# Three helpers of a float32 decoder block: five matmuls whose completion TensorE no longer waits for

## The reference

```python
hs = concatenate([meta, x])                                   # 272 x 2048
hs = hs + 0.5 * swiglu(rmsnorm(hs, ffn1_norm), w_gate1, w_up1, w_down1)     # width 5632
h  = rmsnorm(hs, mix_norm)
u  = h @ w_in + b_in                                          # 2048 -> 5 x 1024: b, c, v, a, g
y_sc = b * causal_dwconv(c * v, conv_sc_w)                    # 3 taps
z    = causal_dwconv(a * sigmoid(g), conv_cf_w) + conv_cf_b   # 31 taps
y_cf = silu(layernorm(z, ln_cf_g, ln_cf_b))                   # over 1024 channels
hs = hs + concatenate([y_sc, y_cf]) @ w_out
hs = hs + 0.5 * swiglu(rmsnorm(hs, ffn2_norm), w_gate2, w_up2, w_down2)
out = rmsnorm(hs, final_norm)[16:]

def rmsnorm(x, g):      return x * rsqrt(mean(x * x) + 1e-6) * g
def layernorm(x, g, b): return (x - mean(x)) * rsqrt(var(x) + 1e-6) * g + b
def swiglu(h, wg, wu, wd): return (silu(h @ wg) * (h @ wu)) @ wd
```

## Time and profile before

| | |
|---|---|
| median of 3 runs | 1862.93 us (1862.60 to 1865.21) |
| the profiled execution's own time | 1862.93 us |
| its span, first to last instruction | 1861.1 us |
| TensorE (PE) busy | 1848.4 us, 99% |
| VectorE (DVE) busy | 1087.9 us, 58% |
| ScalarE (ACT) busy | 902.9 us, 49% |
| mean granted TensorE clock | 0.999 |

### The profile page before, as it was taken

The page is one execution under the profiler, slowest core; times in us unless marked ns, Lnnn a source line. Parts: engine busy times, 40 slices in busy tenths (PEclk is TensorE's granted clock), DMA queues, the critical chain, the costliest instruction groups (busy, mean ns, idle before and its releaser), DMA issues.

```text
span 1861.1 us, 34888 instructions
## 1 busy us (share of the span) xinstructions
PE 1848.4 (99%) x14425; PEld 1803.5 (97%) x14425; DVE 1087.9 (58%) x1218; ACT 902.9 (49%) x1151; POOL 5.9 (0%) x17
## 2 busy tenths in 40 slices
PE   9999999999999999999999999999999999999998
PEld 8999999999999999999999999999999999988886
DVE  7545445555554454468899987555555555544454
ACT  6443434343433443359988765444444444444443
POOL 1000000000000000000000000000000000000000
PEclk9999999999999999999999999999999999999999
DMA  6655555555555565555656566666666666666664
GB/s 222 193 172 177 173 176 174 175 174 176 175 175 176 175 179 173 180 164 178 182 186 177 182 196 194 199 192 192 192 192 194 194 193 195 214 189 189 194 189 135
DMA packets 283359, 342.29 MB, mean 184 GB/s; under 512 B 10639, under 2 KB 223985, under 8 KB 283152
## 3 DMA queue, kind: packets, MB, share of 16 engines
q1 hardware_dynamic: 282672, 340.44, 59.6%
q10 hardware_dynamic: 320, 0.53, 0.1%
q0 software_dynamic: 288, 0.19, 0.0%
HBM read 339.02 MB, written 2.10 MB: 183 GB/s over the span
## 4 chain that ended last, share of the span: by engine, by line
PE 98%; DVE 1%; DMA 0%; ACT 0%; SPq 0%; issue 0%; DVEq 0%
PE ps L463 28%; PE ps L464 28%; PE ps L465 28%; PE ps L558 4%; PE ps L557 4%; PE ps L556 4%; DMA x_tok<-in_x 0%; DVE w_lo L866 0%; PE ps L425 0%; PE ps L574 0%; DVE zc L1067 0%; PE ps L580 0%; DVE ln_mu L892 0%; SPq L320 0%; PE ps L479 0%; ACT o_tok L852 0%
## 5 line engine op out<-in xcount | busy, mean ns | idle before, releaser
L866 DVE TENSOR_TENSOR w_lo<-raw,w_hi 128x1024 fp32r<-128x1024 f32 x639 | 781.5, 1224 | 711.3 <-ACT w_hi L641 709.3
L641 ACT ACTIVATE w_hi<-raw 128x1024 fp32r<-128x1024 f32 x639 | 677.0, 1061 | 915.5 <-PE ps L465 764.4
L463 PE MATMUL ps<-x_hi,w_hi 128*128 128x272 f32 (+2 forms) x3456 | 976.6, 283 | 1.4 <-DVE x_lo L875 1.2
L464 PE MATMUL ps<-x_lo,w_hi 128*128 128x272 f32 (+2 forms) x3456 | 975.9, 282 | 0.0
L465 PE MATMUL ps<-x_hi,w_lo 128*128 128x272 f32 (+2 forms) x3456 | 972.0, 281 | 0.0
L463 PEld LDWEIGHTS ps<-x_hi,w_hi 128*128 128x128 f32 x3456 | 648.9, 188 | 2.8 <-PE ps L479 1.4
L464 PEld LDWEIGHTS ps<-x_lo,w_hi 128*128 128x128 f32 x3456 | 650.7, 188 | 0.0
L465 PEld LDWEIGHTS ps<-x_hi,w_lo 128*128 128x128 f32 x3456 | 649.7, 188 | 0.0
L464 PE MATMUL ps<-a_lo,w_hi 128*128 128x272 f32 x704 | 202.4, 287 | 0.0
L465 PE MATMUL ps<-a_hi,w_lo 128*128 128x272 f32 x704 | 202.2, 287 | 0.0
L463 PE MATMUL ps<-a_hi,w_hi 128*128 128x272 f32 x704 | 201.9, 287 | 0.0
(11 more groups left out here) (139 smaller groups left out, 828.3 us busy)
## 6 DMA issues: line engine op xcount, KB each, us to landing
raw<-in_ffn_w_up SPq DMA_DIRECT2D x176, 512.0 KB, 4.4
raw<-in_ffn_w_down SPq DMA_DIRECT2D x176, 512.0 KB, 4.8
raw<-in_ffn_w_gate SPq DMA_DIRECT2D x175, 512.0 KB, 4.4
raw<-in_w_in SPq DMA_DIRECT2D x80, 512.0 KB, 3.5
raw<-in_w_out SPq DMA_DIRECT2D x32, 512.0 KB, 4.7
x_tok<-in_x SPq DMA_DIRECT2D x4, 512.0 KB, 7.9
gain_tok<-in_final_norm SPq DMA_DIRECT2D x1, 1024.0 KB, 5.1
out_y<-o_tok SPq DMA_DIRECT2D x2, 512.0 KB, 2.9
```

What stands on the lines that cost most here:

```text
L463: pe.matmul(dst, w_high, act_high, start=first, stop=False)
L464: pe.matmul(dst, w_high, act_low, start=False, stop=False)
L641: act.activation(w_hi[s][:, :], raw[s][:, :], ACT.Copy).then_inc(hi_ready, 1)
L866: dve.tensor_tensor(w_lo[s][:, :], raw[s][:, :], w_hi[s][:, :].bitcast(F32), ALU.subtract).then_inc(lo_ready, 1)
```

## The change

Three lines are taken out, one in `square_sums` and two in `layernorm_sums`. Since `square_sums` is called three times, five waits go. The matmuls, their order and the semaphores that they raise stay, and so do the waits of VectorE on them and TensorE's later waits on what VectorE has read.

```diff
             def square_sums(norm, phase):
                 pe.wait_ge(sum_ready[norm], 5 if norm == "start" else KD)
                 pe.matmul(ps[:, 7, 0:width[phase]], ones[:, :], sq_sum[:, tokens(phase)],
                           start=True, stop=True).then_inc(stats_done[norm], 1)
-                pe.wait_ge(stats_done[norm], 1)
...
                     pe.matmul(ps[:, 0, SEQ:2 * SEQ], ones[:, :], ln_sum[:, :],
                               start=True, stop=True).then_inc(ln_mean_done, 1)
-                    pe.wait_ge(ln_mean_done, 1)
                 if b == 10:
                     pe.wait_ge(ln_var_sum, 1)
                     pe.wait_ge(emptied, banks_before("out_sc", 2))
                     pe.matmul(ps[:, SET, SEQ:2 * SEQ], ones[:, :], ln_sum[:, :],
                               start=True, stop=True).then_inc(ln_var_done, 1)
-                    pe.wait_ge(ln_var_done, 1)
```

## The result

The changed kernel is slower: 1880.01 us (1879.94 to 1882.21, 4 runs) against 1864.07 us, a ratio of 1.0088 with a 95% interval of 1.0073 to 1.0104. The 1864.07 is the middle of four runs that lie in two pairs, 1862.60 and 1862.93, 1865.21 and 1865.26; in the later experiments the kernel before took 1862.6 to 1862.7. The forecast was 1861.6 us, in a range of 1860.5 to 1863.8. The five stalls are gone, and each of the five places is shorter by about what was forecast. But behind the sum matmul of gu2, TensorE went through the rest of the stage at a slower pace, and that cost 18 us.

What follows compares the result with a forecast made beforehand. TensorE, busy 1848.4 of 1861.1 us, was taken as the bound. Gains of 0.97 us (gu1, ag, gu2) plus 0.325 (out_sc) made 1.30 off 1862.93, so 1861.6 us, range 1860.5 to 1863.8.

Steps and rivals of the forecast that it cites:

- The working of one site: At each of the five sum matmuls, the stretch from first pass to L464 shortens by 0.325 us, 1.63 in all.
- The three points that could have taken something away: At each site: met wait costs nothing, float32 to fp32r no price, load may not pass ahead; bounds 0 and 0.49 us.
- Rival A: At the five sites the gap stays, since load or matmul can't start before the second pass ends: 1862.7 us, chance 0.10.
- after it TensorE has no wait until the end: Behind gu2's sum matmul TensorE waits for nothing, so that site's 0.325 us reaches the end.
- a loss below zero has no mechanism here: no instruction is added or moved: At one site, the gain was taken as at least 0 and at most 0.49 us.
- the 0.325 that L603 should have come earlier: In out_sc, L603 comes 0.325 us earlier, so VectorE's L1060 starts near 1070.83; of two sites, one counts.
- the waits for `w_lo`, forecast to grow from 0.82 to 1.15 us: At the end of out_sc, the gain behind L603 ends in TensorE's longer wait for VectorE's two `w_lo` blocks.
- The start at 1083.26: TensorE's start after the `w_lo` waits in out_sc, set by VectorE; it moves by what L1060 moves, 0.325 us.
- rival B: In out_sc VectorE swallows more: only gu2 counts, 1862.6 us, or three sites count, 1862.0; chance 0.13 together.
- The prediction's own sign of rival B, a move of less than 0.8: The forecast is wrong by B if TensorE's start near 1083 moves by less than 0.8.
- C: Rival: the granted clock falls to half after out_sc's longer `w_lo` wait; 6 us at that level gives 1867.6; chance 0.02.
- the chance of 0.03 for slower: For the whole kernel, slower by more than 0.2% got 0.03, faster by more 0.03, within 0.94.

Runs made afterwards that it cites:

- experiment 1: The changed kernel with the wait behind the sum matmul of gu2 put back, the other four still away: 1861.95 us, ratio 0.9978.
- experiment 12: The kernel before with only the waits in gu1 and ag taken out: 1861.76 us, ratio 0.9995.
- experiment 6: The kernel before with gu2's wait moved one block later, where it is already met: 1880.98 us, ratio 1.0098.
- experiment 2: The kernel before with only the wait behind the sum matmul of gu2 taken out: 1880.58 us, ratio 1.0098.
- experiment 3: The changed kernel plus one stall on TensorE's own matmul after block 5 of gu2's first group: 1862.16 us in one run, 1880.06 to 1882.43 in four.
- experiment 8: The changed kernel plus stalls behind blocks 4 to 7 of gu2's first group: five runs 1863.45 to 1863.75 us, five 1881.21 to 1881.72.
- experiment 9: The kernel before plus one plain float32 matmul of 128 columns after block 5 of gu2's first group, nobody waiting: 1862.82 us, ratio 0.9995.
- experiment 4: The kernel before plus one plain float32 matmul of 256 columns after block 5 of gu2's first group, nobody waiting: 1881.21 us, ratio 1.0100.
- experiment 10: The kernel before plus two plain float32 matmuls of 256 columns after block 5 of gu2's first group, nobody waiting: 1863.42 us, ratio 1.0004.
- experiment 16: The changed kernel with gu2's sum matmul issued twice in a row, nobody waiting: 1862.09 us, ratio 0.9995 against the kernel before.
- experiment 13: The kernel before with gu2 reading its moving operand from tiles with rows of 272, as stage b does: 1876.69 us, ratio 1.0073.
- experiment 14: The changed kernel with gu2's moving operand 192 bytes lower: 1889.93 us, ratio 1.0143.
- experiment 15: The kernel before, all waits kept, with gu2's moving operand 192 bytes lower: 1891.85 us, ratio 1.0154.

## Why the prediction was wrong

**The working of one site was right.** Forecast 0.325 us for each; the stretch went from 0.91 to 0.58 and from 0.87 to 0.54, so 0.33. The three points that could have taken something away (a met wait, the passage from float32 to fp32r, the load ahead of the pass) took nothing from the site itself. Rival A, and with it the rule of the Trainium skill ("TensorE: Matmul & The Clock Gate", "Part 3: Packing small matmuls — row/col tiling") that a load overlaps matmuls in flight only where row groups differ, is refuted a second time: the load at 1139.75 starts inside a pass that lasts until 1140.13, both over all 128 rows.

**The failing step is the next one**, "after it TensorE has no wait until the end", and with it "a loss below zero has no mechanism here: no instruction is added or moved". The sum carried gu2 as 0.325 us won and the 4128 matmuls behind the site at nothing; measured, they took 18.3 us more. I took the distance of 0.113 us as a property of a 256-column matmul. The profile before held two rows that speak against that, and I did not ask about them. Stage b has 256 columns as well and ran slower. TensorE's stretches of stage b and of the start of out_sc, before:

```profile
1018.00:1038.00 20.00, 20.00 (x172) 1.00 0.60 184
1042.00:1054.00 12.00, 12.00 (x108) 1.00 0.37 113
```

20 us with 172 matmuls and 12 us with 108, less two or three for the edges: 118 and 114 ns: same engine, same clock, same columns, two paces. A kernel that is bound by TensorE to 98% has its time in the product of pace and count, and a change near the stream should be asked first whether it can touch the pace. 4.5 ns is 4% of a pace, and the stage has 4128 matmuls behind the site.

**out_sc.** There too the wait's absence led into the slow pace. In the changed kernel the distances between the mean's matmul and the variance's are at 118 ns (1068.49 to 1069.20 are six in 0.71 us):

```profile
1068.49 0.28 PE L463 MATMUL ps<-y_both,w_hi 128*128 128x256 f32 x1
...
1069.20 0.28 PE L463 MATMUL ps<-y_both,w_hi 128*128 128x256 f32 x1
...
1069.55 0.59 PE L601 MATMUL ps<-ln_sum,ones 128*128 128x256 f32 x2
...
1070.18 0.42 DVE L1057 TENSOR_SCALAR step<-ps 128x256 f32<-128x256 f32 x1 [0.46 <-PE ps L601]
```

So the 0.325 that L603 should have come earlier were eaten on the way: 96 matmuls x 4.5 ns = 0.43. VectorE's wait for it did not shrink (0.35 before, 0.46 after). Behind L603 the stream stayed at 118 ns, which took up what that site gave, until TensorE waited for `w_lo`; behind those waits it was fast again. The count of matmuls from 1072 to 1079 us and from 1084 to 1100 us was 65 and 143 before; after:

```profile
1072.00:1079.00 7.00, 6.93 (x59) 1.00 0.56 193
1084.00:1100.00 16.00, 16.00 (x144) 1.00 0.77 250
```

So the waits for `w_lo`, forecast to grow from 0.82 to 1.15 us, did not grow:

```profile
1078.69 0.19 PEld L463 LDWEIGHTS ps<-y_both,w_hi 128*128 128x128 f32 x1 [0.27 <-DVE w_lo L863]
1082.29 0.19 PEld L463 LDWEIGHTS ps<-y_both,w_hi 128*128 128x128 f32 x1 [0.77 <-DVE w_lo L863]
```

By the weight loads' records they are 1.0 us in all before and 0.27 + 0.77 = 1.04 after. (The 0.82 of the prediction adds a load's idle time, 0.24, to a matmul's, 0.58.) What these two waits did, and the prediction did not foresee, was to end the slow pace in out_sc after seven blocks; gu2 has no such wait.

The start at 1083.26 moved to 1082.29, 0.97 us, which looks like the forecast of 0.975 to the digit, and is not. The changed kernel's profiled run was 0.41 ahead already at the first sum matmul (34.73 against 35.14), before any edit takes effect, because the first load of `x` landed sooner (4.84 us instead of 5.24). Net of that, 0.56 were won until there: the two sites in gu1 and ag (0.65), less 0.1 from out_sc (0.325 - 0.43). The prediction's own sign of rival B, a move of less than 0.8, is passed by the 0.97 and not by the 0.56. Experiments 1 and 12 agree: with gu1 and ag alone 0.9 was won, with both waits of out_sc gone as well 0.7. Two starts in two runs are compared only after what separates the runs before the first edit is taken off.

**Between 1083 and gu2** nothing was won or lost: gu2's sum matmul starts at 1139.54 instead of 1140.50, 0.96 earlier. From there the 18.3 us are lost.

**The same in all traces.** out_sc is a second place to look at, and eighteen traces show it. Its block 6, ahead of the first sum matmul there, starts in all of them with a first distance 0.03 to 0.06 us longer than usual (1055.62 to 1055.77 in experiment 6, 1056.11 to 1056.26 before), and in six of them (2, 3, 6, 8, 9, 12) the rest of the block is at 118 ns, in the twelve others it is at 113 or back there within a few matmuls. No edit stands ahead of this place in experiments 2, 6 and 9. Behind a sum matmul of out_sc with its wait the pace was fast in 23 of 24 cases, and four of the five streams that came to it slow left it fast (2, 9, 12 and, at the variance's, 6); behind one without it the pace was slow in 10 of 12 cases. The one slow case with a wait is experiment 6, behind the mean's matmul; before and there:

```profile
1061.00:1070.00 9.00, 9.00 (x82) 1.00 0.59 199
```

```profile
1060.00:1069.00 9.00, 9.00 (x78) 1.00 0.65 208
```

So the wait makes the fast pace likely and not certain, and a break of 0.04 us is enough to change it.

**The rivals.** B (VectorE swallows more) describes out_sc rightly in its result, three sites instead of four, but for another reason. C, the only slower case, was a fall of the granted clock; it is 1.00 in every stretch of gu2 and 0.999 over the span. "A loss below zero has no mechanism" was a statement about the instruction list, and the chance of 0.03 for slower rested on it.

**What is shown and what is open.** Shown: two steady paces at this operand position (experiments 2, 4 and 6, and 8 within one run); that one removed wait carries the whole loss (1, 2); that a stall, not the waiting instruction, separates the two (6); that a break in the rhythm of another shape gives the other pace (9, 10, 16), and a stall can go both ways (3, 8); that the pace depends on where the moving operand lies (13 to 15), though not on that alone (13). Open: what inside the chip makes a pace of 118 hold for 470 us; and why the stall behind the sum matmul of gu2 led to the fast pace in 79 of 82 runs of the kernel before, to judge by their times, while stalls behind a block did so in 6 of 15 (experiments 3 and 8). The two are not alike: the weight load stood idle for 0.46 to 0.49 us in the first and for 0.25 or 0.26 in four of the five that were traced of the second, and the stream reached the first at the fast pace and the second at either. The three runs in 82 of the kernel before at 1883 us fit the slow pace in size, but no trace of one was taken, so that is argued and not shown.

## What to carry to other kernels

Where TensorE bounds a kernel, compute the distance between matmul starts for each stage and compare stages of the same width: unequal distances with no wait and a full clock are a gain or a loss that no list of waits shows. A wait that looks superfluous may be what starts a long steady stream in its better pace, as gu2's did here, so a change next to such a stream has to be measured over the stream, not over the wait. And a kernel whose runs fall into two groups should be profiled in both before single microseconds are counted.

## What the runs showed of the hardware that was not expected

- A stream of weight load and 256-column fp32r matmul has steady distances of 113, 117, 118 or 120 ns at the same granted clock, by the position of the moving operand and by how the stream was last interrupted; 113 and 118 occur at one and the same position (gu2's tiles, and out_sc's too).
- A pace, once taken, held for the 4128 matmuls of gu2 (851 or 852 in every 100 us), through loop turns and group changes.
- At 272, 260 and 512 columns, and in stage b, a stall changed nothing (125, 119, 228 and 118 ns, one trace with a stall in each).
- One plain float32 matmul or one transposition amid the stream cost 18 us, two plain float32 matmuls 0.8, and one of 128 columns 0.2, which is within the interval of no change.
